# Splitting the float32 projections of a fused kernel's prologue into three float32r products

## The reference, cut to what matters

```python
h = modulate(rmsnorm(x, norm_mix_g), ada[0], ada[1])      # the same for the 256 context tokens
p = h @ w_in + b_in                                       # k, q, v, o, the hyena inputs, gates, merge gates
y_a = hyena_branch(p[hyena part], ...)                    # short convolution, two long convolutions
y_b, state = mlstm_branch(p[q, k, v, o], gates, ...)      # state first built from the context
y = (g_a * (y_a @ w_branch_hy) + g_b * (y_b @ w_branch_ml)) @ w_out
x = x + ada[2] * y
```

## Time and profile before

| | |
|---|---|
| median of three runs | 2400.56 us |
| the profiled execution | 2399.33 us, span 2397.5 us |
| TensorE busy | 2026.2 us (85%), mean granted clock 0.916 |
| VectorE, ScalarE, GpSimd busy | 823.2, 596.3, 0.2 us |
| DMA | 660.82 MB, mean 276 GB/s |

### The profile page before, as it was taken

One profiled execution on the slowest core, in us unless ns is written; L12 is line 12 of the kernel. 1 busy time (PEld: TensorE's weight loads), 2 busy tenths in 40 slices (PEclk: granted clock), 3 DMA queues, 4 the chain that ended last, 5 costly groups with the idle time before them and its releaser, 6 DMA issues.

```text
span 2397.5 us, 28400 instructions
## 1 busy us (share of the span) xinstructions
PE 2026.2 (85%) x12394; PEld 1414.0 (59%) x12394; DVE 823.2 (34%) x1053; ACT 596.3 (25%) x698; POOL 0.2 (0%) x4
## 2 busy tenths in 40 slices
PE   7999997666666667666666899999999999989998
PEld 3586673222222222222222799888999999888998
DVE  4423523000000000000001655566555555557554
ACT  3311201000000000000001433563434433554333
POOL 0000000000000000000000000000000000000000
PEclk9999998888888877778888899999999999999999
DMA  9137255999999999999999445434544545434542
GB/s 395 71 145 329 88 236 216 436 429 432 433 430 432 433 429 434 431 429 434 431 429 430 156 180 197 185 124 152 199 176 176 224 176 195 186 120 150 197 181 97
DMA packets 34092, 660.82 MB, mean 276 GB/s; under 512 B 3784, under 2 KB 4296, under 8 KB 6224
## 3 DMA queue, kind: packets, MB, share of 16 engines
q1 hardware_dynamic: 31984, 651.60, 66.0%
q10 hardware_dynamic: 2016, 7.84, 0.9%
HBM read 658.38 MB, written 1.05 MB: 275 GB/s over the span
## 4 chain that ended last, share of the span: by engine, by line
PE 63%; DMA 29%; DVE 5%; ACT 2%; issue 1%; SPq 0%; ACTq 0%; DVEq 0%
PE ps L1329 62%; DMA ring_b<-experts_dram 19%; DMA ring<-experts_dram 9%; PE ps L1338 1%; DVE ring_lo L1104 1%; ACT w_hi L579 1%; DVE mixer_area L1254 0%; DVE att_area L1250 0%; ACT att_area L700 0%; ACT expert_area L558 0%; DVE tail L942 0%; DVE u_lo L1145 0%; DVE tail L949 0%; ACT u_hi L610 0%; DVE area_h L1084 0%
## 5 line engine op out<-in xcount | busy, mean ns | idle before, releaser
L1104 DVE TENSOR_TENSOR ring_lo<-ring,w_hi 128x2048 fp32r<-128x2048 f32 x168 | 384.9, 2292 | 242.0 <-ACT w_hi L579 242.0
L1329 PE MATMUL ps<-u_hi,w_hi 128*128 128x256 f32 x1536 | 435.5, 284 | 0.0
L1329 PE MATMUL ps<-u_hi,ring_lo 128*128 128x256 f32 x1536 | 432.8, 282 | 0.0
L1329 PE MATMUL ps<-u_lo,w_hi 128*128 128x256 f32 x1536 | 432.0, 281 | 0.0
L579 ACT CAST w_hi<-ring 128x2048 fp32r<-128x2048 f32 x168 | 320.0, 1905 | 201.5 <-PE ps L1329 200.4
L1329 PEld LDWEIGHTS ps<-u_lo,w_hi 128*128 128x128 f32 x1536 | 291.5, 190 | 1.8
L1329 PEld LDWEIGHTS ps<-u_hi,w_hi 128*128 128x128 f32 x1536 | 289.7, 189 | 2.5 <-issue 0.7
L1329 PEld LDWEIGHTS ps<-u_hi,ring_lo 128*128 128x128 f32 x1536 | 289.5, 188 | 0.0
L1329 PE MATMUL ps<-ring,area_h 128*32 128x512 f32 (+1 forms) x1088 | 185.3, 768 | 70.4 <-DMA ring<-experts_dram 62.6
L1329 PE MATMUL ps<-ring_b,area_h 128*32 128x512 f32 x1024 | 160.9, 792 | 81.0 <-DMA ring_b<-experts_dram 72.6
L558 ACT COPY expert_area<-ps 128x1024 f32<-128x1024 f32 x16 | 16.2, 1012 | 616.3 <-PE ps L1329 616.3
(11 more groups left out here) (311 smaller groups left out, 2126.6 us busy)
## 6 DMA issues: line engine op xcount, KB each, us to landing
ring<-stream_dram SPq DMA_DIRECT2D x116, 2048.0 KB, 8.0
ring_b<-experts_dram SPq DMA_DIRECT2D x48, 4096.0 KB, 31.0
ring<-experts_dram SPq DMA_DIRECT2D x48, 4096.0 KB, 31.0
area_n<-norm_rows_dram ACTq DMA_DIRECT2D x6, 512.0 KB, 4.5
tail<-filt_out_dram SPq DMA_DIRECT2D x1, 1536.0 KB, 6.5
tables<-tabs_dram ACTq DMA_DIRECT2D x1, 1408.0 KB, 13.2
tabs<-tabs_dram ACTq DMA_DIRECT2D x1, 1296.0 KB, 10.4
x_tok<-x_dram SPq DMA_DIRECT2D x1, 1024.0 KB, 9.7
```

Of the source, the lines that this page charges most:

```text
L1104: V.tensor_tensor(ring_lo[:, n % RING, :], ring[:, n % RING, :], upper_part(n).bitcast(F32), ALU.subtract).then_inc(sig("alone_ready") if ...
L1329: ins = M.matmul(out, lhsT, rhs, start=start, stop=stop, **more)
```

## The change

Every projection of the prologue becomes three float32r products. The slots with weights of projections are numbered by *split* i (`FIRST_SPLIT`): splits 0 to 3 are slots 8 to 11 (k, v), 4 to 11 the even slots 12 to 26 (q and hyena, two units each), 12 and 13 slots 30 and 35 (o), 14 to 21 merge, 22 to 25 branches, 26 to 29 output. Modulation slots stand between (`ADA_SLOTS`): one after each of splits 4 to 11, then two a head in the state loop. Two ring places hold upper parts now, so the ring has six places from slot 8 on.

The slot numbers and places:

```diff
+FIRST_RING = 6
+ADA_SLOTS = (tuple(range(8)), tuple(range(13, 29, 2)), (28, 29, 31, 32, 33, 34, 36, 37))
+FIRST_SPLIT = (8, 9, 10, 11) + tuple(range(12, 28, 2)) + (30, 35) + tuple(range(38, FIRST_SLOTS))
+BY_POOL = (0, 1) + tuple(range(12, 28))
+BY_VECTOR = tuple(_i for _i in range(len(FIRST_SPLIT)) if _i not in BY_POOL)
...
+
+def first_place(n):
+    return n if n < RING else (n - RING) % FIRST_RING
+
+
+def first_turn(n):
+    return 0 if n < RING else 1 + (n - RING) // FIRST_RING
+
+
+HEAD_UNITS = ((25, 26), (27,), (28, 29), (30,))
...
+        def first_upper(i):
+            if i % 3:
+                return ring_lo[:, FIRST_RING - 1 + i % 3, :]
+            return x_r[:, :] if i < 24 else area_hr[:, SLOT:]
```

SP's loads:

```diff
-                for i in range(PAIRS):
-
-                    sp.wait_ge(sig("slot_used"), rev * RING + (2 * i + 2 - RING))
-                    load(i, rev * PAIRS + i)
+            for i in range((FIRST_SLOTS - RING) // 2):
+
+                sp.wait_ge(sig("slot_used"), 2 * i + (2 if i < 3 else 4))
+                if 2 * i + 4 == FIRST_SPLIT[21] + 1:
+                    sp.dma_start(x_tok[:, :, :], d["x"]).then_inc(sig("x_loaded"), 16)
+                load(i % 3, PAIRS + i)
```

ACT's queue (x is loaded again because `x_r` lies over it):

```diff
+            def upper_first(i):
+
+                n = FIRST_SPLIT[i]
+                act.wait_ge(sig(f"pair_loaded{first_place(n) // 2}"), first_turn(n) * 16 + 16)
+                if i == 0:
+                    act.wait_ge(sig("norm_ready"), TT)
+                elif i < 3:
+                    act.wait_ge(sig("slot_used"), RING)
+                else:
+                    act.wait_ge(sig("slot_used"), FIRST_SPLIT[i - 3] + 1)
+                A.copy(first_upper(i), ring[:, first_place(n), :]).then_inc(sig("first_hi"), 1)
+
+            upper_first(0)
+            upper_first(1)
+            act.wait_ge(sig("mod1_ready"), 1)
+            for k in range(KD):
+                act.wait_ge(sig("hT_ps"), k + 1)
+                for i, out in enumerate((xT[0], cT[0])):
+                    last = A.activation(out[:, k, :], bank(4 + (k + 1) % 4)[:, i * T:(i + 1) * T], ACT.Identity,
+                                        scale=mod1[:, i, k:k + 1], bias=ada_cols[:, i, k:k + 1])
+                last.then_inc(sig("hT_hi"), 1)
+            upper_first(2)
             act.dma_start(vbias[:, :], d["vbias"]).then_inc(sig("biases_loaded"), 16)
...
+            for h in range(H):
+                to_conv(h, col("b_k", h), 2 * T)
+                if h == 1:
+                    upper_first(3)
...
+            upper_first(4)
...
             for h in range(H):
                 act.wait_ge(sig("conv_done"), h + 1)
                 A.activation(kT[:, h, :], kT[:, h, :], ACT.Silu).then_inc(sig("k_ready"), 1)
+            upper_first(5)
+            for i in range(8):
+                upper_first(6 + i)
+                for c in (4 + 2 * i, 5 + 2 * i):
+                    to_conv(c, col("b_q", c - 4) if c < 8 else col("b_hy", c - 8), T)
             for h in range(H):
                 act.wait_ge(sig("conv_done"), 4 + h + 1)
                 A.activation(qT[:, h, :], qT[:, h, :], ACT.Silu).then_inc(sig("q_ready"), 1)
+
             for h in range(H):
-                b = unit_ready(9 + h)
+                b = unit_ready(21 + h)
                 A.activation(oT[:, h, :], b[:, 0:T], ACT.Sigmoid, bias=col("b_o", h)).then_inc(sig("unit_kept"), 1)
-            for c in range(12):
-                to_conv(13 + c, 8 + c, col("b_hy", c), T)
-
-            act.wait_ge(sig("gcols_ps"), 1)
-
-            def merge_gates(*units):
+                act.wait_ge(sig("intra_ps"), h + 1)
+                A.copy(states[:, 2 * h:2 * h + 2, :],
+                       bank(6)[:, 0:2 * VW].rearrange("p (s e) -> p s e", s=2)).then_inc(sig("inter_kept"), 1)
+                if h != 1:
+                    upper_first((14, None, 15, 16)[h])
+
...
+                if h % 2:
+                    upper_first(17 + h // 2)
+                merge_gates(*HEAD_UNITS[h], of=ACT.Identity)
...
                 if o == 0:
+                    merge_gates(31, of=ACT.Identity)
                     act.wait_ge(sig("hsum_ready"), 1)
                     A.activation(hstat, hstat, ACT.Sqrt, scale=1.0 / P, bias=col("eps")).then_inc(sig("hrms_ready"), 1)
-                    merge_gates(33, 34, 35, 36)
+                    upper_first(19)
+                    act.wait_ge(sig("unit_kept"), 32)
+                    A.activation(area_n[:, 0:7 * T], area_n[:, 0:7 * T], ACT.Sigmoid)
+                    merge_gates(32, 33)
+                    upper_first(20)
+                    merge_gates(34)
+                    upper_first(21)
+                    merge_gates(35)
                 else:
-                    merge_gates(37, 38, 39, 40)
+                    merge_gates(36)
+                    upper_first(22)
+                    merge_gates(37, 38)
+                    upper_first(23)
+                    merge_gates(39, 40)
+                    act.wait_ge(sig("slot_used"), FIRST_SPLIT[21] + 1)
+                    act.wait_ge(sig("hm_ready"), 2)
+                    A.copy(y_r[0][:, 4:8, :], oT).then_inc(sig("hT_hi"), 1)
+            upper_first(24)
+            act.wait_ge(sig("z_done"), ORDERS)
+            A.copy(y_r[0][:, 0:4, :], hy_b).then_inc(sig("hT_hi"), 1)
+            upper_first(25)
+            upper_first(26)
+            upper_first(27)
 
             act.wait_ge(sig("grow_ps"), 1)
             A.copy(grow, ps[:, 4:6, :].rearrange("p b n -> p (b n)")).then_inc(sig("grow_ready"), 1)
+            upper_first(28)
+            upper_first(29)
```

DVE's queue: the exact tokens (`exact`), their lower parts, the lower parts of splits 2 to 11, 28 and 29, and the branches' gating:

```diff
+            for k in range(KD):
+                dve.wait_ge(sig("hT_hi"), 1 + k + 1)
+                for i in range(2):
+                    last = V.tensor_scalar(exact[:, i, k, :], bank(4 + (k + 1) % 4)[:, i * T:(i + 1) * T],
+                                           mod1[:, i, k:k + 1], ada_cols[:, i, k:k + 1], ALU.mult, ALU.add)
+                last.then_inc(sig("hT_tmp"), 1)
+            dve.wait_ge(sig("hT_tmp"), KD)
+            for i, v in enumerate((xT, cT)):
+                for k in range(KD):
+                    V.tensor_tensor(v[1][:, k, :], exact[:, i, k, :], v[0][:, k, :].bitcast(F32),
+                                    ALU.subtract).then_inc(sig("hT_lo"), 1)
+            dve.wait_ge(sig("hT_lo"), 1 + 2 * KD)
...
+            lower_first(5)
+            for i in range(8):
+                if 6 + i < 12:
+                    lower_first(6 + i)
+                for c in (4 + 2 * i, 5 + 2 * i):
+                    if c < 8:
+                        short_conv(c, qT[:, c - 4, :], col("ml_conv", 3 * (c - 4), 3), (on_x,))
+                    else:
+                        short_conv(c, hy(c - 8), col("hy_conv", 3 * (c - 8), 3), (on_x,))
             dve.wait_ge(sig("gcols_ps"), 1)
...
+            step(V.tensor_copy(gcols, bank(6)[:, 0:64].rearrange("p (n s t h) -> p n s t h", n=4, s=2, t=TT)))
             V.tensor_scalar(gcols[:, 1], gcols[:, 1], QSCALE, None, ALU.mult).then_inc(sig("gcols_ready"), 1)
             dve.wait_ge(sig("gcols_ready"), 1)
+            ada_row(1, 4)
 
 
...
+                if o == 1:
+                    dve.wait_ge(sig("hT_hi"), 1 + KD + 1)
+                    V.tensor_tensor(y_r[1][:, 4:8, :], oT, y_r[0][:, 4:8, :].bitcast(F32),
+                                    ALU.subtract).then_inc(sig("hT_lo"), 1)
...
+            dve.wait_ge(sig("hT_hi"), 1 + KD + 2)
+            V.tensor_tensor(y_r[1][:, 0:4, :], hy_b, y_r[0][:, 0:4, :].bitcast(F32),
+                            ALU.subtract).then_inc(sig("hT_lo"), 1)
             dve.wait_ge(sig("unit_kept"), 41)
             for k in range(KD):
                 dve.wait_ge(sig("branch_ps"), k + 1)
                 m = merge[:, k, :, :].rearrange("p g t -> p (g t)")
-                step(V.tensor_tensor(m, bank(k % 4), m, ALU.mult))
-                V.tensor_tensor(merge[:, k, 0, :], merge[:, k, 0, :], merge[:, k, 1, :],
-                                ALU.add).then_inc(sig("merged"), 1)
+                total = expert_area[:, 2048 + k % 2 * T:2048 + (k % 2 + 1) * T]
+                V.tensor_tensor(m, bank(k % 4), m, ALU.mult).then_inc(sig("gated"), 1)
+                dve.wait_ge(sig("gated"), k + 1)
+                step(V.tensor_tensor(total, merge[:, k, 0, :], merge[:, k, 1, :], ALU.add))
+                step(V.tensor_copy(merge_r[:, k, 0, :], total))
+                V.tensor_tensor(merge_r[:, k, 1, :], total, merge_r[:, k, 0, :].bitcast(F32),
+                                ALU.subtract).then_inc(sig("merged"), 1)
 
```

GpSimd's program:

```diff
+        @block.gpsimd
+        def _(pool):
+            for i in BY_POOL:
+
+                pool.wait_ge(sig("first_hi"), i + 1)
+                at = first_place(FIRST_SPLIT[i])
+                nc.gpsimd.tensor_tensor(ring_lo[:, at, :], ring[:, at, :], first_upper(i).bitcast(F32),
+                                        ALU.subtract).then_inc(sig("first_lo_p"), 1)
```

(135 more changed lines are left out.)

318 lines of the change are left out of this document (139 added, 179 removed).

## The result

The changed kernel takes **2422.99 us** (median of 4 runs, 2420.72 to 2423.18) where the kernel before takes 2399.86 on the same chip: ratio 1.0093, 95% interval 1.0081 to 1.0106, 23 us slower. The forecast was 2406, in a range of 2389 to 2416. The sign is right, and the size is off by 17 us.

The account below looks back on a forecast made before the run. TensorE's own matmuls were taken to bound the prologue. Matmuls saved 44.9 us; late loads, start, branches, output, clock and port added back more, summing to +5.6 us: 2406 on the median, range 2389 to 2416.

Parts of the forecast that it names:

- Groups: Eight prologue groups of two units and one modulation slot: 6.67 us each, with loads and splitting hidden, 0.8 us to spare.
- (a): Late load of slots 30-31 for split 12, around the gate transposes: TensorE waits, +6.5 us.
- (b): State loop, h = 0: split 13's cast waits for slot 35 ahead of the last convolutions, delaying kw: +15.6 us.
- the port: VectorE instructions reading two SBUF tensors wait for GpSimd subtractions: between 0 and 14 us, middle taken, +7.
- (c): State loop: split 14's cast waits for slots 38-39, holding the states copy of h = 1: +10.0 us.
- (d): Heads: split 16's cast delays the first exponential; TensorE idle 3.5 us instead of 1.4: +2.1 us.
- The clock behind (a) to (c): After each of these waits some 5 us of TensorE work run at half rate, 2.5 us lost each: +7.5 us.
- Full exclusion: Rival: GpSimd and two-input VectorE work exclude each other at every place, port cost at upper end: 2413; chance 0.22.
- Start: Prologue start: ScalarE casts sixteen pieces instead of eight, TensorE idle 2.3 us against 1.7: +0.5 us.
- without clock and port: Rival: half clock and GpSimd beside VectorE cost nothing: 2392; chance 0.15.
- without (b): Rival: slot 35 has landed and been cast before h = 0 is done, so no kw wait: 2386; chance 0.12.
- starved groups: Rival: 2 MB loads under the casts take over 9 us, so each of the eight groups waits: 2414; chance 0.11.

Follow-up runs that it names:

- E1: Changed kernel with ScalarE's cast of split 13 moved from ahead of the last two convolutions to behind the first states copy: 2411.79 us, ratio 1.0043.
- E2: Changed kernel with all four ScalarE casts of the state loop (splits 13 to 16) moved behind what they held up: 2405.78 us, ratio 1.0016.
- E7: Changed kernel with extra products filling TensorE's waits at (a), (b) and (c), 50, 145 and 68 of them: 2418.19 us, ratio 1.0071.
- E3: Changed kernel with splits 25 to 27, in the branches, subtracted by VectorE instead of GpSimd: 2407.81 us, ratio 1.0031.
- E4: Changed kernel with splits 12 and 13 subtracted by VectorE instead of GpSimd, ScalarE's order kept: 2414.65 us, ratio 1.0055.
- E8: Changed kernel with 50 products added ahead of branch 6, in TensorE's wait for VectorE: 2415.87 us, ratio 1.0062.
- E12: Changed kernel with E9's start change alone, but 9 float32 products instead of 19: 2418.13 us, ratio 1.0068.
- E9: Changed kernel with the second weight cast behind the first hT casts and 19 float32 products before the first sweep: 2422.24 us, ratio 1.0086.
- E5: Changed kernel with E2, E3 and E4's splits together, split 13 behind kw of h = 1: 2391.05 us, ratio 0.9957.
- E6: E5 with splits 14 to 24 subtracted by VectorE too, GpSimd keeping only splits 0 and 1: 2386.20 us, ratio 0.9942.
- E10: E6 with E9's start, modulation slots of h = 0 and 2 ahead of their unit, lower parts 16 and 17 later: 2384.94 us, ratio 0.9935.
- E11: E10 with 9 products instead of 19, and split 12's cast and lower part behind the last convolutions: 2375.65 us, ratio 0.9894.

## Why the prediction was wrong, point by point

**Right.** The matmuls within some 2 us (see Groups), the four late loads and their places. (a): 5.9 us of idle against 6.5. (b): 18.6 against 15.6, and 4.0 more for the port, which makes 19.6. (c): 9.2 against 10.0. The cause of (b) and (c) is shown by E1 and E2; (d) was moved only together with the others. The clock behind (a) to (c) was put at 7.5 and E7 makes it 5 to 8. State loop and heads together came out 2.1 under the terms: the four loads took 7.3 to 7.5 us where the prediction took 8.2, 3.2 less in all, and an instruction held in head 1 cost 3.3 where it had 1.7. z came out 2.2 under. The groups' loads stayed hidden, and GpSimd took 4.5 to 4.85 us a split where I had taken 4.6.

**The step that failed most: "No row leans, so I take the middle: +7."** The port is all or nothing, and it was all. The true choice was 0 or 14, and the middle was a time that neither case gives: "Full exclusion", at 0.22, was the mechanism (E3, E4). Even its 2413 would have been 10 us short. Its price was short by 2.5 us in the branches. I gave them 6.7 for two held instructions, and counted only those that read two SBUF tensors; three were held, the cast among them, and TensorE idled 6.0 and then ran at half clock for 2.6 (E8).

**"Start. +0.5."** It was 6.8 in this execution; in E1 to E8, with the same start, the second sweep came up to 1.1 us earlier. The first product came 1.8 us later (46.59 against 44.82), and gates and k, 28.5 by cadence, lasted 33.5 (46.59 to 80.10). The term compared amounts of idle time and left out their place: ScalarE could cast nothing before its load landed at 41.8, had two slots to cast ahead of the first hT piece, and TensorE idled 4.9 us and ran at half clock after it. E12 gave 1.2 to 2.3 us back by the order of the casts and by filling the wait; the rest is ScalarE's and VectorE's chain through sixteen pieces, which I argue and did not test.

**"Clock. After each of (a), (b) and (c)."** The branches' wait had no clock term, nor had anything behind it: 2.6 and 3.9 us (E8).

**Groups.** "24 x 0.119 = 2.85 us" is the cadence inside a run; a unit took 2.97 in place (6.94 a group instead of 6.67). Eight groups: +2.1.

Together, for the execution that was profiled: 5.6 + 7 (port) + 6.3 (start) + 2.1 (groups) + 2.5 (branches) + 3.8 (the stretch with the router) - 2.1 - 2.2 = 23.0, against 23.1 measured.

The other rivals: without clock and port (2392) and without (b) (2386) fell with the waits list; starved groups fell with 94.45 us of TensorE without a gap in the chain and loads of 7.3 to 8.6 us under the groups.

## What to carry to other kernels

A cast that waits for a load stops everything behind it on its engine: put it behind what others wait for, and price a late load by the queue and not by its own consumer. A cost that is a lock has two values; forecast one of them, and list who reads SBUF on both engines, casts and one-input instructions too, before giving GpSimd work beside VectorE. The stall in the branches cost its 6.0 us of idle time plus 2.6 at half clock behind it, and 50 products in the wait bought the second part back; look for a bank that is free by then (E7) and count how long they last (E9).

## What was not expected of the hardware

- One VectorE instruction passes between two GpSimd subtractions that are queued up, so three instructions of together 1.1 us took 13.4 us (4.16, 4.60, 4.60), a one-input cast among them, while one that reads PSUM and one SBUF tensor kept its 0.68. The exclusion holds both ways: a subtraction that began during VectorE's 0.43 us was 0.2 to 0.3 longer.
- With the stall in the branches TensorE's clock halved once more 40 us later, at the router: 9.1 to 9.6 us in all runs with the stall (the changed kernel, E1, E2, E4, E7, E9, E12), 5.21 in E3 and E8, which had no idle TensorE there, and 6.9 in E5, E6, E10 and E11. The last show that it is no matter of the stall alone; why it comes so late stays open.
- A 2 MB load landed in 7.3 to 7.5 us at (a) to (d), where it ran alone or nearly so, and in 14.7 us at the start (27.12), with others under way.
